# Prompt attention: scaled probabilities turned, values loaded for two heads and both groups, branches summed in PSUM, keys in four pieces

## The chip, the cores and the metric

One Trainium2 chip, one core. The metric is the device time of one execution in microseconds (us), as a median over runs; lower is better.

## The reference, cut to what matters

One inference step of a decoder layer on 1024 prompt tokens and 64 sample tokens. The part that changes is the sparse attention of the prompt: 8 query heads of width 64 in two groups of four, each group with its own keys and values, and three branches whose outputs are mixed with gates. With the top 16 of 16 blocks chosen, the selected branch of the prompt sees all earlier keys.

```python
def nsa_core(q, q_pos, kc, vc, ks_blk, vs_blk, kw, vw, kw_pos, gates, rel_bias):
    logit_c = einsum('bqgrd,bkgd->bgrqk', q, kc) * scale + bias      # 63 compressed keys
    p_c = masked_softmax(logit_c, dist_c >= 0)
    o_cmp = einsum('bgrqk,bkgd->bqgrd', p_c, vc)
    ...
    p_s = masked_softmax(logit_s, dist_s >= 0)                       # selected: all earlier keys
    o_slc = einsum('bgqnr,bgqnd->bqgrd', p_s, v_sel)
    ...
    p_w = masked_softmax(logit_w, mask_w)                            # window: the last 512 keys
    o_win = einsum('bgrqk,bkgd->bqgrd', p_w, vw)
    return gates[..., 0:1] * o_cmp + gates[..., 1:2] * o_slc + gates[..., 2:3] * o_win
```

The sum of the three is normalised and goes through an output projection that is added to x. Feed-forward layers, a state-space branch, a memory attention and the same attention for the sample tokens stand around it.

## The kernel before

The kernel is a row of stages, each a block of its own in which the five engines run side by side and at whose end they meet. `prompt_nsa_stage` stands between `scan_and_compress_stage` and `sample_nsa_stage`; after them comes `gemm_stage` "wout", the output projection that adds to x (`add_to=x`).

**Units.** The stage works in 8 tiles i of 128 queries. A unit u is one tile, one head (group g, head r of the group) and one branch b: b=0 is the selected branch over key tiles 0..i, b=1 the window branch over at most the last 5 key tiles, with the 63 compressed keys beside it. That makes 16 units a tile and 128 in all. Within a tile the order is head r, then group g, then branch b.

**A unit's path.** `scores(u)` on TensorE multiplies the packed queries by the keys split in a high and a low part (L2204, L2205) and adds biases with identity matmuls (L2211 near table, L2214 window mask, L2218 to L2222 compressed keys and their bias), into one of two halves of `s_ps`. VectorE takes the maximum (L2356, L2358). ScalarE takes the exponential with its sum (L2310, L2313) into `prob`, of which there are two. `turn(u)` transposes it by 128x128 pieces (L2233, L2236) into `t_ps`, of which there is one. ScalarE and VectorE copy it to `prob_t` (L2324 to L2329, L2369, L2371). `values(u)` multiplies: the turned probabilities are the loaded operand (128 columns), the values of one group move (64 columns), once for each key tile (L2251) and once for the compressed keys (L2255). The three branches of a head land side by side in `o_ps`. VectorE's `weights` forms gate/sum for the three, and `combine` scales and adds them into `o` (L2402, L2406). Once a tile, `turn_output` transposes `o` (L2264) and ScalarE copies it to `o_t` (L2334).

**Orders.** TensorE goes turn(u), scores(u+2), values(u-1); ScalarE exp(u+1), copy(u); VectorE maxima(u+1), copy(u), and after each b=1 unit weights and combine. Ahead of the first scores all tables and all keys are split (`to_split`, L2296 on ScalarE, L2420 on VectorE), and TensorE waits for the last of them. SyncE issues the loads: keys of the selected branch, near table, queries of tile 0, compressed bias, keys of the window branch, compressed keys, mask, queries of tile 1, then x itself (`x_back`: x had been put aside in DRAM, since its tile serves the scan stage), then further queries.

**The matmuls of `values`** are in plain fp32, and each of them stands in the trace as two records (a weight load and a matmul for each half of the operand). Those of `scores` are in the rounded fp32 type and stand as one.

## Time and profile before

| what | us |
|---|---|
| median of 3 runs (range) | 3262.19 (3257.46 to 3265.14) |
| the profiled execution, span from first to last instruction | 3261.7 |
| prompt attention, first scores to last output copy | 1542.9 to 1964.2 |
| TensorE busy in the whole span | 2881.9 (88%) |
| VectorE, ScalarE busy in the whole span | 1604.9 (49%), 983.2 (30%) |

The only time that the trace states for the profiled execution is its span, so the span stands for it. PE is TensorE's matmuls, PEld its weight loads, DVE VectorE, ACT ScalarE, SP SyncE. A busy PE is not a PE at its peak: matmuls overlap, so the distance between starts is read, not the duration of one. PEclk is the clock that was granted, 1.00 for 2.4 GHz and 0.50 for 1.2 GHz.

### The profile page before, as it was taken

The page shows a single profiled execution, that of the slowest core. Times are in us where ns is not written, and L with a number is a line of the kernel's source. Part 1 is how long each engine was busy: PE and PEld are TensorE (multiplying, and loading weights), DVE is VectorE, ACT ScalarE, POOL GpSimd, SP SyncE. Part 2 cuts the span into 40 slices and gives each one's busy share as a digit, 9 for nine tenths or more (in the row PEclk, how much of TensorE's full clock was granted, in tenths as well). Part 3 has the DMA queues.
Part 4 walks back from the last instruction along what each step waited for, and adds up shares of the span by engine and source line. Part 5 has one row for each costly group of instructions (what it writes and reads, how often), then busy time and mean ns, then how long its engine had stood idle before and what let it go on. Part 6 is the DMA issues. An engine that isn't in the chain of part 4 may idle for free. (4 is left out here: it accounts for less than half of the span.)

```text
span 3261.7 us, 49905 instructions
## 1 busy us (share of the span) xinstructions
PE 2881.9 (88%) x20104; PEld 2749.7 (84%) x20104; DVE 1604.9 (49%) x2976; ACT 983.2 (30%) x2029; POOL 117.4 (4%) x118
## 2 busy tenths in 40 slices
PE   5999999999799849994999995697475999999998
PEld 5999999999799849984999993496365999999997
DVE  6766766441631132433445552524337766666433
ACT  4333333211431221212344441412333333334111
POOL 5000000000000000000000000000005000000000
PEclk9999999999899966987579997798687999999999
DMA  2222224210342430204000005100201222224111
GB/s 85 80 80 78 73 77 148 106 67 1 111 54 58 151 112 12 72 27 147 20 14 8 1 1 147 40 27 27 88 19 39 75 77 74 77 80 174 67 67 56
DMA packets 121208, 221.37 MB, mean 68 GB/s; under 512 B 14388, under 2 KB 75860, under 8 KB 119508
## 3 DMA queue, kind: packets, MB, share of 16 engines
q1 hardware_dynamic: 116004, 207.88, 20.6%
q10 hardware_dynamic: 4976, 10.31, 0.8%
q8 instruction: 161, 2.64, 0.3%
q14 instruction: 67, 0.55, 0.1%
HBM read 172.85 MB, written 49.36 MB: 68 GB/s over the span
## 5 line engine op out<-in xcount | busy, mean ns | idle before, releaser
L740 PE MATMUL ffn_gate_up<-ffn_h_hi,ffn_w 128*128 128x272 f32 x1912 | 560.6, 293 | 60.4 <-DVE ffn_h_lo L881 42.0
L741 PE MATMUL ffn_gate_up<-ffn_h_lo,ffn_w 128*128 128x272 f32 x1912 | 558.0, 292 | 0.0
L742 PE MATMUL ffn_gate_up<-ffn_h_hi,ffn_w 128*128 128x272 f32 x1912 | 557.4, 292 | 0.0
L740 PEld LDWEIGHTS ffn_gate_up<-ffn_h_hi,ffn_w 128*128 128x128 f32 x1912 | 365.3, 191 | 65.8 <-DVE ffn_h_lo L881 32.0
L742 PEld LDWEIGHTS ffn_gate_up<-ffn_h_hi,ffn_w 128*128 128x128 f32 x1912 | 365.2, 191 | 0.0
L741 PEld LDWEIGHTS ffn_gate_up<-ffn_h_lo,ffn_w 128*128 128x128 f32 x1912 | 365.2, 191 | 0.0
L1073 DVE SCALAR_TENSOR_TENSOR x<-ffn_down,x 128x364 f32<-128x364 f32 (+1 forms) x240 | 126.1, 533 | 329.1 <-PE ffn_down L309 329.1
L886 DVE TENSOR_TENSOR ffn_w<-ffn_w_raw,ffn_w 128x512 fp32r<-128x512 f32 x264 | 186.6, 709 | 104.4 <-ACT ffn_w L621 104.4
L621 ACT ACTIVATE ffn_w<-ffn_w_raw 128x512 fp32r<-128x512 f32 x264 | 160.1, 625 | 99.3 <-PE ffn_down L742 79.2
L740 PE MATMUL ffn_down<-ffn_h_hi,ffn_w 128*128 128x272 f32 x552 | 163.7, 297 | 13.4 <-DVE ffn_w L886 7.9
L1479 PE MATMUL ssd_hid_ps<-ssd_pages,ssd_cmp_w 128*128 128x128 f32 (+1 forms) x1280 | 171.2, 298 | 0.0
L307 PE MATMUL mix_ps<-h_mix_hi,mix_w_hi 128*128 128x364 f32 x480 | 161.4, 336 | 9.4 <-issue 6.0
L1479 PEld LDWEIGHTS ssd_hid_ps<-ssd_pages,ssd_cmp_w 128*128 128x128 f32 x1280 | 163.8, 211 | 2.6
L741 PE MATMUL ffn_down<-ffn_h_lo,ffn_w 128*128 128x272 f32 x552 | 162.1, 294 | 0.0
L742 PE MATMUL ffn_down<-ffn_h_hi,ffn_w 128*128 128x272 f32 x552 | 161.9, 293 | 0.0
L309 PE MATMUL mix_ps<-h_mix_hi,mix_w_lo 128*128 128x364 f32 x480 | 160.0, 333 | 0.0
L308 PE MATMUL mix_ps<-h_mix_lo,mix_w_hi 128*128 128x364 f32 x480 | 160.0, 333 | 0.0
L2251 PE MATMUL pn_o_ps<-nat,pn_prob_t 128*128 128x64 f32 x1056 | 154.3, 294 | 0.0
L2251 PEld LDWEIGHTS pn_o_ps<-nat,pn_prob_t 128*128 128x128 f32 x1056 | 145.5, 212 | 0.0
L2310 ACT ACTIVATE pn_prob<-pn_s_ps,pn_neg_max 128x640 f32<-128x640 f32 (+7 forms) x128 | 89.9, 702 | 182.4 <-DVE pn_neg_max L2358 125.0
L307 PE MATMUL ffn_down<-ffn_h_hi 128*128 128x364 f32 (+1 forms) x384 | 126.2, 329 | 0.0
L309 PE MATMUL ffn_down<-ffn_h_hi,ffn_h_lo 128*128 128x364 f32 (+1 forms) x384 | 126.1, 328 | 0.0
(492 smaller groups left out, 6564.6 us busy)
## 6 DMA issues: line engine op xcount, KB each, us to landing
ffn_w_raw<-in_w_ffn_in SPq DMA_DIRECT2D x88, 512.0 KB, 4.1
scratch_ffn_act<-ffn_prod SPq DMA_DIRECT2D x88, 272.0 KB, 2.6
ffn_h_raw<-scratch_ffn_act SPq DMA_DIRECT2D x44, 544.0 KB, 7.2
mix_w_raw<-in_w_mix SPq DMA_DIRECT2D x20, 512.0 KB, 3.6
ffn_h_raw<-in_w_ffn_out SPq DMA_DIRECT2D x16, 512.0 KB, 9.1
ssd_pages<-in_cmp_pages SPq DMA_DIRECT2D x64, 128.0 KB, 2.2
sn_slc_pages<-in_slc_pages SPq DMA_DIRECT2D x64, 128.0 KB, 2.2
ffn_w_sum<-in_w_ffn_out SPq DMA_DIRECT2D x14, 512.0 KB, 11.1
```

What stands on the lines that cost most here:

```text
L307: pe.matmul(out, w_hi, x_hi, start=start, stop=False)
L308: pe.matmul(out, w_hi, x_lo, start=False, stop=False)
L309: return pe.matmul(out, w_lo, x_hi, start=False, stop=stop)
L621: act.activation(w[:, a, 0, :], fresh(a), ACT.Copy).then_inc(w_hi_ready, 1)
L740: pe.matmul(out, hi, x_hi, start=start, stop=False, skip_group_check=chained)
L741: pe.matmul(out, hi, x_lo, start=False, stop=False, skip_group_check=chained)
L742: mm = pe.matmul(out, lo, x_hi, start=False, stop=stop, skip_group_check=chained)
L886: dve.tensor_tensor(w[:, a, 1, :], fresh(a), w[:, a, 0, :].bitcast(F32), ALU.subtract).then_inc(w_ready, 1)
L1073: dve.scalar_tensor_tensor(xT[:, t, cols], dn_bank(d), 0.5, xT[:, t, cols], ALU.mult, ALU.add).then_inc(dn_added, 1)
L1479: mm = pe.matmul(hp[j % 2][:, 1 - later:1 - later + w].rearrange("p (b n) -> p b n", n=PAGES), w1s[:, kv, k, hh * P:(hh + 1) * P], pages[: ...
L2251: mm = pe.matmul(at, probt[:, u % 2, m * P:(m + 1) * P], nat[:, j, vcol:vcol + HEAD_DIM], start=m == 0, stop=m == len(kt) - 1)
L2310: e = act.activation(prob[:, u % 2, 0:w], s[:, 0:w], ACT.Exp, bias=neg_max[:, u % 2, 0:1], accum_out=sums[:, n % 2, 1 + b:2 + b])
```

## The change

It touches the prompt attention alone, and where x is loaded again.

- The probabilities of a unit are scaled by gate/sum on VectorE (`scale`: a reciprocal and a tensor_scalar with two per-row factors, for b=1 two of them) before they are turned. `weights`, `combine`, `o` and `turn_output` go.
- Eight units make a set: one tile, two heads r of each group, both groups, both branches. Turned probabilities of a set are kept in 14 slots (8 selected key tiles, 5 window key tiles, 1 compressed), in one of two buffers, the second of which is the tile of x.
- `values` loads the 64 columns of values of one group and moves 256 columns (two heads), for group 0 into PSUM partitions 0 to 63 and for group 1 into 64 to 127; all slots of a set add up in one PSUM tile. The matmuls of a set are issued in up to 7 portions behind the turns of the next set's units. ScalarE copies the finished set from `o_ps` into `o_t`.
- TensorE's order is scores(u+2), turn(u), portion; turn is cut in two with a signal each; VectorE takes maxima two units ahead. `prob` has three buffers. First copies of the turned pieces go to VectorE for b=0 units of group 0 and to ScalarE for the others, further pieces to ScalarE.
- Keys come and are split in four pieces of 256 tokens, the near table in two halves. The first scores wait for the first pieces alone, the second unit for the compressed tables, the second set for the second half of the near table. Queries are loaded into one buffer.
- `x_back` moves from the prompt stage's SyncE queue to the end of the sample stage's.

```diff
@@ prompt_nsa_stage: tiles @@
-        prob = sb("prob", [P, 2, 1024])
-        probt = sb("prob_t", [P, 2, 1024])
+        prob = sb("prob", [P, NB, 1024])
         neg_max = sb("neg_max", [P, 2, 2])
-        sums, rec, mix = sb("sums", [P, 2, 3]), sb("rec", [P, 2, 3]), sb("mix", [P, 2, 3])
-        o = sb("o", [P, 2, INNER])
-
+        sums, rec = sb("sums", [P, NB, 2]), sb("rec", [P, NB, 2])
...
+        half = SLOTS * 4 * P
+        own_probt = sb("prob_t", [P, half])
+        probt = [a.rearrange("p (n g r t) -> p n g r t", n=SLOTS, g=KV_GROUPS, r=2)
+                 for a in (own_probt[:], spare[:, 0:half])]
...
+        near_raw = spare[:, 0:H * 2 * P].rearrange("p (g v r c) -> p g v r c", g=KV_GROUPS, v=2, r=2)
...
+        def piece_at(u):
+            i, j = divmod(u, per_tile)
+            return (j // 8, (i + 1) // 2) if i % 2 and j % 8 == 2 and (i + 1) // 2 < PIECES else None
+        def key_piece(a, n, p):
+            return a[:, n, :].rearrange("p (g t) -> p g t", g=KV_GROUPS)[:, :, p * PIECE:(p + 1) * PIECE]
+        near_pair = lambda v: (near_raw[:, :, v], by_pairs(near_hi)[:, :, v], by_pairs(near_lo)[:, :, v])
+        NEAR0, EYE, CMPB, KC, WIN, NEAR1 = range(6)
+        tables = [(*near_pair(0), near_landed[0], 32), (core.ident, eye[:], None, None, 0),
+                  (cmpb, cmpb_hi[:], cmpb_lo[:], filled, 5), (kc_raw, kc_hi[:], kc_lo[:], kc_landed, 64),
+                  (win_raw, win[:], None, win_landed, 16), (*near_pair(1), near_landed[1], 32)]
+        split_count = {NEAR0: 1, CMPB: 2, KC: 3, NEAR1: 4}
...
+        has_rest = [len(key_tiles(u)) > 4 or units[u][3] == 1 for u in range(U)]
+        rests_before = [sum(has_rest[:u]) for u in range(U + 1)]
+        first_on_dve = [units[u][3] == 0 and units[u][1] == 0 for u in range(U)]
@@ sync @@
+                load_keys(0, 0)
+                load_q(0)
+                load_near(0)
+                load_keys(1, 0)
...
-                x_back(sp)
-                for i in range(2, tiles):
-                    load_q(sp, i)
+                load_near(1)
+                for i in range(1, tiles):
+                    load_q(i)
+                    if i % 2 and (i + 1) // 2 < PIECES:
+                        for n in range(2):
+                            load_keys(n, (i + 1) // 2)
@@ tensor @@
+                    if u % per_tile < 2 and i % 2 == 0:
+                        pe.wait_ge(k_ready[b], i // 2 + 1)
+                    if u == 0:
+                        pe.wait_ge(split_done, split_count[NEAR0])
+                        pe.wait_ge(hi_done, EYE + 1)
+                    if u == 1:
+                        pe.wait_ge(split_done, split_count[KC])
+                    if u == SET:
+                        pe.wait_ge(split_done, split_count[NEAR1])
+                        pe.wait_ge(hi_done, len(tables))
...
+                    pe.wait_ge(scaled, u + 1)
+                    if u:
+                        wait_first_copy(pe, u - 1)
...
-                    kt = key_tiles(u)
-                    at = o_ps[:, n % 2, (1 + b) * HEAD_DIM:(2 + b) * HEAD_DIM]
-                    vcol = b * P + g * HEAD_DIM
-                    for m, j in enumerate(kt):
-                        mm = pe.matmul(at, probt[:, u % 2, m * P:(m + 1) * P], nat[:, j, vcol:vcol + HEAD_DIM],
-                                       start=m == 0, stop=m == len(kt) - 1)
...
+                def values(s, steps, last):
+                    for n, (slot, b, j) in steps:
+                        for g in range(KV_GROUPS):
+                            gs = slice(g * HEAD_DIM, (g + 1) * HEAD_DIM)
+                            if b is None:
+                                vg = (DEC_BATCH * 2 + g) * HEAD_DIM
+                                v, keys = vc[:N_CMP, vg:vg + HEAD_DIM], N_CMP
+                            else:
+                                vg = b * P + g * HEAD_DIM
+                                v, keys = nat[:, j, vg:vg + HEAD_DIM], P
+                            mm = pe.matmul(o_ps[gs, s % 2, 0:2 * P], v,
+                                           probt[s % 2][:keys, slot, g].rearrange("p r t -> p (r t)"),
+                                           start=n == 0, stop=n == last)
+                    return mm
+                def some_values(s, k):
+                    slots = slots_of(s)
+                    steps = list(enumerate(slots))[len(slots) * (k - 1) // (SET - 1):len(slots) * k // (SET - 1)]
+                    if k == 1:
+                        pe.wait_ge(pt_act, act_copies[(s + 1) * SET])
+                        pe.wait_ge(pt_dve, dve_copies[(s + 1) * SET])
+                        if s >= 2:
+                            pe.wait_ge(o_done, s - 1)
+                    if steps:
+                        mm = values(s, steps, len(slots) - 1)
+                        if k == SET - 1:
+                            mm.then_inc(pv_ready, 1)
...
+                    turn(u)
+                    s, k = divmod(u, SET)
+                    if s and k:
+                        some_values(s - 1, k)
+                for k in range(1, SET):
+                    some_values(sets - 1, k)
@@ scalar @@
+                def take_output(s):
+                    i, v = divmod(s, 2)
+                    act.wait_ge(pv_ready, s + 1)
+                    act.activation(o_t[:, 2 * v:2 * v + 2, i * P:(i + 1) * P],
+                                   o_ps[:, s % 2, 0:2 * P].rearrange("p (r t) -> p r t", t=P), ACT.Copy
+                                   ).then_inc(o_done, 1)
...
+                    if u == 0:
+                        round_table(WIN)
+                        round_table(NEAR1)
+                    if u % SET == 0 and u >= 2 * SET:
+                        take_output(u // SET - 2)
@@ vector @@
+                def scale(u):
+                    i, g, r, b = units[u]
+                    h, w = g * GROUP_HEADS + r, len(key_tiles(u)) * P
+                    mine = prob[:, u % NB]
+                    dve.wait_ge(p_ready, u + 1)
+                    dve.reciprocal(rec[:, u % NB, 0:1 + b], sums[:, u % NB, 0:1 + b]).then_inc(rec_ready, 1)
+                    dve.wait_ge(rec_ready, u + 1)
+                    m = dve.tensor_scalar(mine[:, 0:w], mine[:, 0:w], rec[:, u % NB, 0:1], gates[:, i, h, 1 + b:2 + b],
+                                          ALU.mult, ALU.mult)
                     if b:
-                        w = min(n, 4) * P
-                        dve.tensor_copy(probt[:, u % 2, 0:w], t_ps[:, 0, 0:w]).then_inc(pt_dve, 1)
-                    elif n > 4:
-                        dve.tensor_copy(probt[:, u % 2, 4 * P:n * P], t_ps[:, 1, 0:(n - 4) * P]
-                                        ).then_inc(pt_dve, 1)
-                def weights(n):
-                    i, g, r, _ = units[2 * n]
-                    h = g * GROUP_HEADS + r
-                    dve.wait_ge(p_ready, 2 * n + 2)
-                    dve.reciprocal(rec[:, n % 2, :], sums[:, n % 2, :]).then_inc(rec_ready, 1)
-                    dve.wait_ge(rec_ready, n + 1)
-                    mixed = dve.tensor_tensor(mix[:, n % 2, :], rec[:, n % 2, :], gates[:, i, h, :], ALU.mult)
-                    if i == 0:
-                        mixed.then_inc(mix_ready, 1)
-                        dve.wait_ge(mix_ready, 2 * n + 1)
-                        mixed = dve.tensor_tensor(mix[:, n % 2, 0:1], mix[:, n % 2, 0:1], core.sees_cmp[:],
-                                                  ALU.mult)
-                    mixed.then_inc(mix_ready, 1)
...
-                def combine(n):
-                    i, g, r, _ = units[2 * n]
-                    at = o[:, i % 2, (2 * r + g) * HEAD_DIM:(2 * r + g + 1) * HEAD_DIM]
-                    dve.wait_ge(mix_ready, mix_count(n))
-                    dve.wait_ge(pv_ready, 2 * n + 2)
-                    if i >= 2:
-                        dve.wait_ge(ot_ps, i - 1)
-                    for k in range(3):
-                        part = o_ps[:, n % 2, k * HEAD_DIM:(k + 1) * HEAD_DIM]
-                        if k == 0:
-                            dve.tensor_scalar(at, part, mix[:, n % 2, 0:1], None, ALU.mult
-                                              ).then_inc(part_ready, 1)
-                        else:
-                            dve.wait_ge(part_ready, 2 * n + k)
-                            dve.scalar_tensor_tensor(at, part, mix[:, n % 2, k:k + 1], at, ALU.mult, ALU.add
-                                                     ).then_inc(part_ready if k == 1 else o_ready, 1)
+                        own = mine[:, 5 * P:5 * P + N_CMP]
+                        m = dve.tensor_scalar(own, own, rec[:, u % NB, 1:2], gates[:, i, h, 0:1], ALU.mult, ALU.mult)
+                    m.then_inc(scaled, 1)
...
+                maxima(1)
+                scale(0)
                 for u in range(U):
                     if u % per_tile == pack_at and u + per_tile < U:
                         pack(units[u][0] + 1)
+                    if piece_at(u):
+                        rest_keys(*piece_at(u))
+                    if u + 2 < U:
+                        maxima(u + 2)
+                    copy(u)
+                    if u == 0:
+                        rest_table(NEAR1)
                     if u + 1 < U:
-                        maxima(u + 1)
-                    copy(u)
-                    if units[u][3]:
-                        weights(u // 2)
-                        if u > 1:
-                            combine(u // 2 - 1)
-                combine(U // 2 - 1)
+                        scale(u + 1)
@@ sample_nsa_stage, sync, and trunk @@
                for bt in range(PAIRS):
                    load(bt)
+                x_back(sp)
...
+            prompt_nsa_stage(core, nat, kc, vc, o["proj"], rows, o_t, x[:].rearrange("p k t -> p (k t)"))
+            sample_nsa_stage(core, nat, kc, vc, o["proj"], rows, i["rules"], i["page_table"],
+                             i["slc_pages"], i["win_kv"], gates_dram, o_t, n_pool,
```

## Rows read from the trace of the kernel before

**Rows 1.** The page: the granted clock in 40 slices of 81.5 us, in tenths:

```profile
PEclk9999999999899966987579997798687999999999
```

**Rows 2.** Windows of the prompt attention: length, busy (records), PEclk, DMA share, GB/s; sum of ten:

```profile
1578.00:1626.00 48.00, 47.22 (x216) 44.97 (x216) 20.68 (x76) 17.55 (x69) 0.00 (x0) 0.50 0.05 12
...
1674.00:1724.00 50.00, 47.04 (x364) 43.84 (x364) 30.64 (x89) 24.48 (x77) 0.00 (x0) 1.00 0.05 12
...
sum 454.00, PE 412.27 PEld 391.25 DVE 234.91 ACT 190.51 POOL 1.48; mean PE 41.23 PEld 39.12 DVE 23.49 ACT 19.05 POOL 0.15
```

**Rows 3.** Groups in the stretch 1480 to 2060: busy us, mean ns, idle before:

```profile
L2251 PE MATMUL pn_o_ps<-nat,pn_prob_t 128*128 128x64 f32 x1056 | 154.3, 294 | 0.0
...
L2233 PE MATMUL pn_t_ps<-const_all,pn_prob 128*128 128x128 f32 x528 | 92.6, 302 | 8.6 <-ACT mixed L2334 5.5 <-ACT pn_prob L2313 2.2 <-issue 0.7
L2356 DVE TENSOR_REDUCE pn_neg_max<-pn_s_ps 128x1 f32<-128x640 f32 (+7 forms) x128 | 90.1, 704 | 64.3 <-PE pn_s_ps L2211 61.5 <-PE pn_s_ps L2222 2.3
...
L2369 DVE COPY pn_prob_t<-pn_t_ps 128x512 f32<-128x512 f32 (+3 forms) x64 | 37.8, 591 | 85.1 <-PE pn_t_ps L2236 85.1
L2406 DVE SCALAR_TENSOR_TENSOR pn_o<-pn_o_ps,pn_mix,pn_o 128x64 f32<-128x64 f32 x128 | 36.3, 284 | 4.6
L2324 ACT ACTIVATE pn_prob_t<-pn_t_ps 128x512 f32<-128x512 f32 (+3 forms) x64 | 33.1, 517 | 4.1 <-PE pn_t_ps L2233 3.7
L2255 PE MATMUL pn_o_ps<-vc,pn_prob_t 63*128 63x64 f32 x128 | 32.7, 343 | 0.0
...
L2402 DVE TENSOR_SCALAR pn_o<-pn_o_ps,pn_mix 128x64 f32<-128x64 f32 x64 | 18.1, 284 | 1.7 <-PE pn_o_ps L2255 1.4 <-DVE pn_mix L2381 0.3
...
L2264 PE MATMUL pn_t_ps<-const_all,pn_o 128*128 128x128 f32 x32 | 5.8, 312 | 1.1 <-DVE pn_o L2406 1.1
```

**Rows 4.** The values in the slow stretch, by line:

```profile
1542.00:1674.00 132.00, 40.40 (x155) 37.86 (x156) 0.50 0.13 39
```

**Rows 5.** Timeline of TensorE in tile 7, clock 1.00: start, length, records:

```profile
1949.67 1.22 PE L2251 MATMUL pn_o_ps<-nat,pn_prob_t 128*128 128x64 f32 x10
1950.82 0.43 PE L2255 MATMUL pn_o_ps<-vc,pn_prob_t 63*128 63x64 f32 x2
1951.18 0.77 PE L2233 MATMUL pn_t_ps<-const_all,pn_prob 128*128 128x128 f32 x5
```

**Rows 6.** Timeline of TensorE in the memory attention, clock 0.50:

```profile
2340.38 0.41 PE L3027 MATMUL ma_s_ps<-ma_k_lo,ma_q_prompt 128*128 128x256 f32 x1
2340.73 1.98 PE L3047 MATMUL ma_o_ps<-ma_prob_t,ma_v 128*64 128x128 f32 x16
```

**Rows 7.** Windows around 512-column matmuls in the sample attention:

```profile
2008.00:2010.00 2.00, 1.96 (x12) 0.58 (x16) 0.00 (x0) 0.00 (x0) 0.00 (x0) 0.50 0.52 147
2012.00:2014.00 2.00, 2.00 (x23) 0.93 (x21) 0.00 (x0) 0.00 (x0) 0.00 (x0) 1.00 0.42 134
```

**Rows 8.** Timeline of the start of the prompt attention:

```profile
1515.27 2.47 SPq L2151 DMA_DIRECT2D pn_raw<-out_proj  x4
...
1522.68 1.91 ACT L2296 ACTIVATE pn_k_hi<-pn_raw 128x2048 fp32r<-128x2048 f32 x1 [17.66 <-DMA pn_raw<-out_proj]
...
1542.92 0.44 PE L2204 MATMUL pn_s_ps<-pn_k_hi,pn_q 128*128 128x128 f32 x1 [31.63 <-DVE pn_cmp_bias_lo L2420]
```

**Rows 9.** VectorE groups by shape, whole span:

```profile
L234 DVE SCALAR_TENSOR_TENSOR wout_norm_normed<-mixed,inner_gains,wout_norm_inv_rms 128x364 f32<-128x364 f32 x24 | 13.8, 595 | 0.6
...
L2784 DVE TENSOR_SCALAR sn_prob<-sn_prob,sn_mix 128x1088 f32<-128x1088 f32 x4 | 3.1, 786 | 0.1
...
L2785 DVE TENSOR_SCALAR sn_prob<-sn_prob,sn_mix 128x576 f32<-128x576 f32 x4 | 2.1, 513 | 0.0
```

**Rows 10.** DMA issues: count, KB each, us to landing:

```profile
x<-scratch_x SPq DMA_DIRECT2D x1, 4368.0 KB, 17.3
```

**Rows 11.** Timeline of SyncE, the last load of the sample attention:

```profile
2042.06 0.43 SPq L2532 DMA_DIRECT2D sn_win_kv<-in_win_kv  x1
```

**Rows 12.** Timeline of VectorE, the first use of x:

```profile
2125.62 0.98 DVE L1198 TENSOR_TENSOR x<-wout_ps,x 128x364 f32<-128x364 f32 x2
```

More of the change, by code:

```diff
@@ L2105, in prompt_nsa_stage @@
         U = len(units)
+        SET = 2 * KV_GROUPS * 2
+        sets = U // SET
+        per_tile = 2 * H
+        pack_at = 6
         def key_tiles(u):
@@ new lines, in prompt_nsa_stage, with rest_copies @@
+        has_rest = [len(key_tiles(u)) > 4 or units[u][3] == 1 for u in range(U)]
+        rests_before = [sum(has_rest[:u]) for u in range(U + 1)]
+        first_on_dve = [units[u][3] == 0 and units[u][1] == 0 for u in range(U)]
+        dve_copies = [sum(first_on_dve[:u]) for u in range(U + 1)]
+        def rest_copies(u):
+            n, b = len(key_tiles(u)), units[u][3]
+            return (n > 4) + b
+        act_copies = [0]
+        for u in range(U):
+            act_copies.append(act_copies[-1] + (not first_on_dve[u]) + rest_copies(u))
@@ new lines, in wait_first_copy, with slots_of, turned @@
+        def wait_first_copy(pe, u):
+            if first_on_dve[u]:
+                pe.wait_ge(pt_dve, dve_copies[u + 1])
+            else:
+                pe.wait_ge(pt_act, act_copies[u] + 1)
+        def slots_of(s):
+            slc, own = key_tiles(s * SET), key_tiles(s * SET + 1)
+            return [(m, 0, j) for m, j in enumerate(slc)] + [(WIN0 + m, 1, j) for m, j in enumerate(own)] + \
+                [(CMP_SLOT, None, None)]
+        def turned(u, first, count, keys=P):
+            i, g, r, b = units[u]
+            base = (WIN0 if b else 0) + first
+            return probt[u // SET % 2][:keys, base:base + count, g, r % 2, :]
@@ L2225, in turn @@
                 def turn(u):
-                    pe.wait_ge(p_ready, u + 1)
-                    pe.wait_ge(pt_act, act_copies[u])
-                    pe.wait_ge(pt_dve, dve_copies[u])
-                    if u % per_tile == turn_at + 1 and units[u][0]:
-                        pe.wait_ge(ot_ready, units[u][0])
-                    for n in range(len(key_tiles(u))):
-                        mm = pe.transpose(t_ps[:, n // 4, (n % 4) * P:(n % 4 + 1) * P],
-                                          prob[:, u % 2, n * P:(n + 1) * P], core.ident[:])
@@ L2269, in _ @@
-                pe.wait_ge(split_done, splits)
+                    b, n = units[u][3], len(key_tiles(u))
+                    pe.wait_ge(scaled, u + 1)
+                    if u:
+                        wait_first_copy(pe, u - 1)
+                    for m in range(min(n, 4)):
+                        mm = pe.transpose(t_ps[:, 0, m * P:(m + 1) * P], prob[:, u % NB, m * P:(m + 1) * P],
+                                          core.ident[:])
+                    mm.then_inc(t_first, 1)
+                    if not has_rest[u]:
+                        return
@@ L2272, in _ @@
                 for u in range(U):
-                    turn(u)
                     if u + 2 < U:
                         scores(u + 2)
-                    if u:
-                        values(u - 1)
-                    if u % per_tile == turn_at and units[u][0]:
-                        turn_output(units[u][0] - 1, u)
-                values(U - 1)
-                turn_output(tiles - 1, U - 1)
+                    turn(u)
[4 more added lines that the diff above has]
+                    some_values(sets - 1, k)
             @block.scalar
@@ L2298, in _ @@
                                ).then_inc(gates_ready, 1)
+                round_keys(0, 0)
+                pack(0)
+                round_table(NEAR0)
+                round_table(EYE)
+                round_keys(1, 0)
                 def exp(u):
-                    i, g, r, b = units[u]
-                    n = u // 2
+                    b = units[u][3]
                     w = len(key_tiles(u)) * P
@@ L2344, in _ @@
                     copy(u)
-                    if u % per_tile == turn_at and units[u][0]:
-                        take_output(units[u][0] - 1)
-                take_output(tiles - 1)
+                    if u == 0:
[3 more added lines that the diff above has]
+                        take_output(u // SET - 2)
+                take_output(sets - 2)
+                take_output(sets - 1)
             @block.vector
```

243 lines of the change are left out of this document (116 added, 127 removed).

## Prediction

> **What bounds the kernel now.** I read the granted clock of the page first [rows 1]. The prompt attention (1543 to 1964) fills the 20th to the 24th of the 40 digits: 5, 7, 9, 9, 9. The stage began at the low clock and kept it for a third of its length (until 1674, near the end of tile 2). The windows say what TensorE did then [rows 2]: in 1578 to 1626 it was busy for 47.2 of 48 us, with 216 matmul records at 0.50; in 1674 to 1724 it was busy for 47.0 of 50 us with 364 at 1.00. So TensorE is never short of work, at either clock, and its own instructions set the stage's length. The other engines are well below: in the ten windows the sums are 412 us for PE, 235 for DVE, 191 for ACT [rows 2]. The groups say what PE does [rows 3]: the values are the largest, 1056 records (L2251) and 128 for the compressed keys (L2255), ahead of 528 transposes. The timelines give the distances that the sum needs: at 1.00 ten values records and the step to the next take 1.15 us, so 0.112 us each [rows 5], though only 64 columns move, with a load of 128 columns before each. Two kinds of waste stand there, a weight load as dear as the matmul, and a low clock.
>
> **Values.** Before: of 1056 records 155 run at 0.50 [rows 4]. The distance there I take as 0.213 us, twice 0.107: the window at 0.50 has 216 records of all kinds in 48 us, 0.22 each [rows 2]. 155 x 0.213 + 901 x 0.112 = 134 us. The compressed keys are another tile shape (63 rows); their groups' busy time, 32.7 us [rows 3], is near what they occupy, since a pair in tile 7 takes 0.36 us (1950.82 to 1951.18) [rows 5] and one at the low clock about twice that. Together 167 us.
>
> After: 3 + 5 + 7 + 9 + 11 + 12 + 13 + 14 = 74 slots a set pair, 148 in all, each with two matmuls (one a group) of 256 columns, four records. What does such a record cost? The trace has the very shape, also with neighbours in different halves of the array's columns: the memory attention's 16 records of 128*64 with 128 columns take 1.98 us at 0.50 [rows 6]. Less a last record's 0.42 that is (1.98 - 0.42) / 7 = 0.22 us for two of them. Twice the columns at twice the clock cost the same, so 0.22 us (I take 0.218) for a pair at 1.00 and 0.43 at 0.50, if the halves work side by side at 256 columns as they do there. Six slots of tile 0 run at 0.50 (12 pairs x 0.43 = 5 us), 142 at 1.00 (284 x 0.218 = 62 us): 67 us.
>
> The change adds a price: each portion of values changes the array's shape from 128*128 to 128*64 and back. Going from 128*128 scores to 128*64 values took 0.35 us from start to start (2340.38 to 2340.73), 0.13 more than a plain step, at 0.50 [rows 6]; a 63-row pair at 1.00 costs 0.36 instead of 0.22, 0.14 for going in and out less what overlaps [rows 5]. There are 3 + 5 + 6 x 7 = 50 portions for each of two sets, 100, so 200 changes; at 0.1 us (bounds 0 and 0.13) 20 us, and 2 for the compressed slot. The Trainium skill has a rule against this change: by TensorEngine Tiling (Array Packing), Key Properties, changing the tiling mode, not merely the tile, drains the engine. It gives no figure, so by the rule alone the term is a loss of unknown size; the 0.13 us of the row agrees.
>
> Values after: 67 + 22 = 89. **Gain 167 - 89 = 78 us.**
>
> **Output turns.** `turn_output` goes: 5.8 us busy and 5.5 us in which transposes waited for the ACT copy [rows 3]. **Gain 10 us** (bounds 6 and 11).
>
> **Clock.** 131 us ran at 0.50 (1543 to 1674), 33 of them values, 14 compressed values (20 pairs at 0.7), 3 output turns; about 81 are scores and transposes. Tile 0 of these is 15 records a unit pair x 8 pairs x 0.213 = 26 us. What did the engine do before its clock rose? Elsewhere it rose within 4 us of full-length 512-column matmuls in quarter tiles (0.50 at 2008, 1.00 at 2012) [rows 7]; in this stage it stayed low through nearly all of tiles 0 to 2, where most matmuls have 64 to 256 columns and each waits for its weight load. Afterwards the values have 256 columns in two halves at once, and they begin with unit 9, in tile 0. I take it that the clock rises some 8 us into tile 1. Then (81 - 26 - 7) / 2 = 24 us are saved. **Gain 24 us**; bounds 0 (rises as late as now) and 40 (rises in tile 0).
>
> **Start.** TensorE's first scores began at 1542.92, 31.6 us after its last work, released by the last table split; the first key load was issued at 1515.27 and its 1 MB landed at 1522.7 [rows 8]. Now the first scores need a quarter of the keys, the queries and half the near table: four instead of nine loads' worth of bytes, about 1527. But unit 1 waits for the compressed bias tables, which still come behind these (about 1531), and at u = 0 ACT and DVE have the second half of the near table in their queues, whose load is issued last, near 1530, and lands some 8 us later as such loads do. Behind it stand exp(2) and scale(1), so turn(1) stalls until about 1539 with only about 5 us of work done ahead. The stage is then 9 us ahead of before. **Gain 9 us** (bounds 4 and 13). The later key pieces (ACT and DVE, two of each every second tile) are the same columns as before, now under TensorE.
>
> **VectorE and ScalarE.** `scale`: 786 ns for 1088 columns, 513 for 576 [rows 9], so 0.206 + 0.533 ns a column. The units have 8 x 128 x (36 + 30) = 67,584 columns in all: 128 x 0.206 + 36 = 62 us, 64 short ones at 0.25 = 16, 128 reciprocals at 0.17 = 21: 99 us. Removed: 36.3 + 18.1 [rows 3] and some 22 of reciprocals and mixes. Copies fall from 37.8 [rows 3] and 16 of a smaller group to 19 us, since only 32 units' first copies (mean 0.59) stay. Net about -11, so 224 us. ACT gets 32 more first copies (0.517 each [rows 3]), 32 further ones and 16 outputs (some 0.4 each) for 8 outputs now, about +32: 223 us. Both have to fit in some 310 us of TensorE. They fit, but no longer loosely, and they are chained: `t_ps` and the two halves of `s_ps` are single per role. In a light tile (tile 1 at 1.00) a pair of units takes PE 2.8 us and DVE about 2.6. I add **10 us of stalls** (bounds 0 and 35, the latter if scaling with two per-row factors goes one column a ns, as a two-input operation does: 364 columns in 595 ns [rows 9], which makes DVE 36 us longer).
>
> **x.** `x_back` took 17.3 us to land [rows 10], issued behind the last sample load (2042.06 [rows 11]); it lands about 2060, the first use is at 2125.6 [rows 12]. 65 us of slack: cost 0. Without that slack it would be 17.
>
> **Sum.** 78 + 24 + 10 + 9 - 10 = 111 us from a span of 3261.7, which is 0.5 below the median of 3262.2. **Forecast 3151.**
>
> **Rivals.**
> 1. The clock rises as late as now, near the end of tile 2. For it: transposes and bias matmuls of at most 256 columns are untouched and make up most of the records. Price: the 24 us, and the 24 slots of tiles 1 and 2 at twice 0.44, 10 more: 3185. 17%.
> 2. VectorE becomes the pace-setter in the light tiles by the slow scaling. Price 15 to 25: 3171. 12%.
> 3. The halves don't overlap at 256 columns. Against it: the 128x64 rows [rows 6]. Price 284 x 0.218 = 62 and 5: 3218. 5%.
> 4. Slower: the clock never rises in the stage. Stalls, shape changes and small matmuls keep it at 0.50 to the end. The stage after is 421 - 111 + 9 = 319 us, of which some 270 at 1.00; at 0.50 they take up to 270 more, less 35 of stalls that vanish and shape changes that don't double: about 3385. It decides once 220 us of work at 1.00 turn slow. Against it: today's stage, with nothing wider in its first tiles, does rise. 5%.
>
> **How the numbers follow.** Forecast 59% (3125 to 3175), rivals 17, 12, 5, 5, something that leaves the time about as it is 2. The range of 8 in 10 reaches down to an early rise and no cost of shape changes (16 and 20 us, 3115) and up over rivals 1 and 2 together (3205). Faster by over 0.2% 0.93, within 0.2% (6.5 us, about what three such runs can tell from no change) 0.02, slower 0.05.
>
> **What would show it.** Values records fall to 592, in pairs started together, 0.22 us apart at 1.00. PEclk reads 0.50 in tile 0 and 1.00 from about 1590. DVE and ACT each about 225 us in the stage. The stage ends near 1853 instead of 1964. Gap to the first scores about 15 us, with a second gap until about 1539. L1198 waits for PE, not for x. Wrong if: PEclk stays at 0.50 past tile 1, pairs stand 0.43 apart at 1.00, TensorE waits for `scale` more than 10 us in all, or wout waits for the x load.

## The result, and the profile after

| | us |
|---|---|
| after, median of 4 runs (range) | 3167.47 (3163.2 to 3173.43) |
| before, median of 4 runs (range) | 3261.59 (3257.46 to 3265.14) |
| after / before | 0.9711, 95% interval 0.9698 to 0.9725 |

The kernel is 94 us faster; the forecast was 111, in its range. The profiled execution of after has a span of 3171.7, the longest of its four, 90.0 below that of before.

The page: totals, and the granted clock in 40 slices of 79.3 us, beside [rows 1]:

```profile
PE 2803.2 (88%) x19480; PEld 2611.3 (82%) x19480; DVE 1598.8 (50%) x2912; ACT 1000.2 (32%) x2108; POOL 117.4 (4%) x118
...
PEclk9999999999899976898699987896678999999999
```

Groups of the stage (1520 to 1868), beside [rows 3]: busy us, mean ns, idle before and its releasers.

```profile
L2284 PE MATMUL pn_t_ps<-const_all,pn_prob 128*128 128x128 f32 x416 | 72.5, 287 | 11.6 <-DVE pn_prob L2463 11.2 <-DVE pn_prob L2459 0.2
L2459 DVE TENSOR_SCALAR pn_prob<-pn_prob,pn_rec,pn_gates 128x640 f32<-128x640 f32 (+7 forms) x128 | 71.0, 555 | 4.7
...
L2309 PE MATMUL pn_o_ps<-pn_prob_t,nat 128*64 128x256 f32 x264 | 39.8, 405 | 0.0
...
L2309 PE MATMUL pn_o_ps<-x,nat 128*64 128x256 f32 x264 | 37.5, 395 | 0.0
...
L2457 DVE RECIPROCAL pn_rec<-pn_sums 128x1 f32<-128x1 f32 (+1 forms) x128 | 19.8, 155 | 1.1 <-ACT pn_prob L2378 0.9
L2463 DVE TENSOR_SCALAR pn_prob<-pn_prob,pn_rec,pn_gates 128x63 f32<-128x63 f32 x64 | 19.7, 308 | 0.0
```

The values, 187 us of busy records before [rows 3], are 264 + 264 records here and 64 more for the compressed keys. In exchange the transposes wait for `scale` (L2459, L2463), 11.4 us in all.

Windows tile by tile, from one tile's first exponential to the next: length, busy (records) of PE, PEld, DVE, ACT and POOL, PEclk, DMA share, GB/s. Tiles 1 and 2 of before, then tiles 0 to 2 and the sum of all eight of after:

```profile
1579.80:1628.00 48.20, 47.42 (x216) 45.17 (x215) 20.67 (x74) 17.26 (x67) 0.00 (x0) 0.50 0.05 12
1628.00:1683.30 55.30, 54.24 (x265) 52.06 (x265) 23.78 (x73) 19.91 (x66) 0.00 (x0) 0.58 0.05 10
```

```profile
1528.50:1563.60 35.10, 29.86 (x129) 25.78 (x130) 18.52 (x70) 16.21 (x72) 0.41 (x2) 0.50 0.24 54
1563.60:1591.70 28.10, 23.47 (x166) 17.43 (x165) 20.78 (x71) 18.43 (x74) 0.00 (x0) 0.99 0.16 39
1591.70:1623.70 32.00, 29.34 (x201) 21.85 (x199) 23.52 (x70) 20.16 (x72) 0.00 (x0) 1.00 0.07 17
...
sum 337.40, PE 319.11 PEld 241.98 DVE 222.75 ACT 201.63 POOL 0.41; mean PE 39.89 PEld 30.25 DVE 27.84 ACT 25.20 POOL 0.05
```

Nearly half of the gain, 43.4 us, comes from tiles 1 and 2 (103.5 to 60.1): they were at the low clock, tile 2 until near its end [rows 2], now they are not. There TensorE now idles, 4.6 and 2.7 us of them, where it was idle for 0.8 and 1.1. The tiles of all kernels (tile 7 up to the end of the last values, in the kernels with the old order up to the last output turn behind them; names as in the experiments below):

```
us of tile            0     1     2     3     4     5     6     7   PEclk, tile 1
before              35.4  48.1  55.4  43.4  54.0  55.9  59.5  67.4   0.50
after               35.1  28.1  32.0  37.2  46.1  47.5  50.3  60.7   0.99
3 portions          35.3  31.1  32.8  40.4  45.0  47.8  48.7  59.5   0.87
1 portion           35.7  31.7  33.5  39.8  45.9  50.3  49.7  58.1   0.79
same half           35.4  30.2  36.2  42.6  53.9  57.3  61.0  79.6   1.00
no scale            35.6  24.8  29.1  34.6  45.0  46.5  49.2  59.2   0.99
fill after          35.0  28.2  32.0  37.2  46.1  47.5  50.2  60.6   0.99
fill before         33.7  41.5  58.7  43.4  54.0  55.9  59.5  67.4   0.66
wait all            30.1  32.5  32.0  37.2  46.1  47.5  50.2  60.6   0.71
one slot            33.0  30.4  32.8  37.2  46.1  47.5  50.2  60.6   0.78
portion first       35.8  31.0  31.6  37.2  45.7  46.8  48.7  58.1   0.89
before, few values  35.4  37.2  37.4  44.8  54.0  55.9  59.5  67.4   0.70
first from tile 4   35.3  28.1  32.0  37.2  46.2  46.8  48.7  58.1   1.00
the same, 4 portions 35.3 32.5  32.0  37.2  46.1  49.8  49.2  58.5   0.76
```

The timeline of TensorE in tile 7 of after, around one portion (start, length, records), beside [rows 5]:

```profile
1819.98 0.27 PE L2292 MATMUL pn_t_ps<-const_all,pn_prob 128*128 128x128 f32 x1
1820.09 0.27 PE L2295 MATMUL pn_t_ps<-const_all,pn_prob 128*63 128x128 f32 x1
1820.29 1.08 PE L2309 MATMUL pn_o_ps<-x,nat 128*64 128x256 f32 x8
1821.31 0.50 PE L2256 MATMUL pn_s_ps<-pn_k_hi,pn_q 128*128 128x512 f32 x1
1821.64 0.39 PE L2257 MATMUL pn_s_ps<-pn_k_lo,pn_q 128*128 128x512 f32 x1
1821.87 0.40 PE L2256 MATMUL pn_s_ps<-pn_k_hi,pn_q 128*128 128x512 f32 x1
1822.11 0.39 PE L2257 MATMUL pn_s_ps<-pn_k_lo,pn_q 128*128 128x512 f32 x1
```

Two transposes stand 0.11 apart, the last one and the first values 0.20: 0.09 for going in. The last portions of the stage stand together, with nothing between them, and show the pair's own price:

```profile
1859.29 5.57 PE L2309 MATMUL pn_o_ps<-x,nat 128*64 128x256 f32 x50
```

(5.57 - 0.38) / 24 = 0.216 us a pair, as forecast. Four such pairs are 0.86; in the portion they take 1.02 (1820.29 to 1821.31), 0.16 more. What the way out costs shows only beside a turn that has no portion behind it, the first of a set:

```profile
1810.53 0.60 PE L2292 MATMUL pn_t_ps<-const_all,pn_prob 128*128 128x128 f32 x4
1810.89 0.48 PE L2256 MATMUL pn_s_ps<-pn_k_hi,pn_q 128*128 128x512 f32 x1
1811.20 0.40 PE L2257 MATMUL pn_s_ps<-pn_k_lo,pn_q 128*128 128x512 f32 x1
```

The four transposes start 0.11 apart, so the last of them at 1810.86 and the first scores only 0.03 behind it. From the last transpose to the second scores matmul it is 0.34 us here, and 1.55 with a portion of four pairs between them (1820.09 to 1821.64). Less 0.86 for the pairs, a portion so costs 0.35 us beside its pairs: 0.09 going in, 0.16 within, 0.10 going out. The forecast had 0.20.

The start and x, from the timeline of after, beside [rows 8, 11, 12]:

```profile
1527.05 0.45 PE L2256 MATMUL pn_s_ps<-pn_k_hi,pn_q 128*128 128x128 f32 x1 [14.96 <-DVE pn_near_bias_lo L2480]
...
1531.48 0.45 PE L2256 MATMUL pn_s_ps<-pn_k_hi,pn_q 128*128 128x128 f32 x1 [3.34 <-DVE pn_kc_lo L2480]
...
1537.75 0.48 PE L2284 MATMUL pn_t_ps<-const_all,pn_prob 128*128 128x128 f32 x1 [1.17 <-DVE pn_prob L2463]
...
1943.82 0.43 SPq L3251 DMA_DIRECT2D x<-scratch_x  x1
...
2030.47 0.54 DVE L1198 TENSOR_TENSOR x<-wout_ps,x 128x364 f32<-128x364 f32 x1
```

x is issued at 1943.8 and lands 14.3 us later, 72 us before its first use; nothing waits for it. The stage's last output copy ends at 1865.9 instead of 1964.2, 98 us earlier. The other 8 us are given back in later stages that the change does not touch: the sample attention (from here to its last combine) takes 111.9 us instead of 107.9, with TensorE's mean clock at 0.69 instead of 0.73, the output projection 0.8 and what follows up to the feed-forward layer 2.7 us more. In eight of the ten other kernels that load x at the new place the sample attention takes 107.3 to 109.3, so its 4.0 us belong to this execution, not to x.

### The profile page after: what moved, and what is told of

The parts are those of the page before. It is cut to its first block and busy times, and to the rows that moved or that the text cites. A ratio compares the mean times of both kernels' runs of the same rounds, so it can differ in the third digit from the quotient of the medians.

```text
span 3171.7 us, 48273 instructions
## 1 busy us (share of the span) xinstructions
PE 2803.2 (88%) x19480; PEld 2611.3 (82%) x19480; DVE 1598.8 (50%) x2912; ACT 1000.2 (32%) x2108; POOL 117.4 (4%) x118
## 5 line engine op out<-in xcount | busy, mean ns | idle before, releaser
L2435 DVE TENSOR_REDUCE pn_neg_max<-pn_s_ps 128x1 f32<-128x640 f32 (+7 forms) x128 | 90.4, 706 | 88.1 <-PE pn_s_ps L2263 49.0
L308 PE MATMUL ffn_down<-ffn_h_lo,ffn_h_hi 128*128 128x364 f32 (+1 forms) x384 | 126.1, 328 | 0.0
L2024 DVE TENSOR_TENSOR mix_w_lo<-mix_w_raw,mix_w_hi 128x1024 fp32r<-128x1024 f32 (+1 forms) x22 | 27.2, 1234 | 190.0 <-ACT mix_w_hi L1958 190.0
```

What stands on the lines that cost most here:

```text
L308: pe.matmul(out, w_hi, x_lo, start=False, stop=False)
L2024: dve.tensor_tensor(w_lo[:, n % 2, 0:w], raw[:, n % 2, 0:w], w_hi[:, n % 2, 0:w].bitcast(F32), ALU.subtract).then_inc(lo_ready, 1)
L2435: m = dve.tensor_reduce(neg_max[:, u % 2, 0:1], s[:, 0:w], AX_X, ALU.max, negate=True)
```

## Experiments

Each ratio is to the kernel before on the same chip; 0.9711 is the changed kernel's own. 0.001 is 3.3 us.

**3 portions a set** (48 instead of 100) and **1 portion a set** (16):

```diff
-  steps = ...[len(slots) * (k - 1) // (SET - 1):len(slots) * k // (SET - 1)]
+  if k not in PORTIONS: return              # (3, 5, 7), or (4,)
+  at, count = PORTIONS.index(k), len(PORTIONS)
+  steps = ...[len(slots) * at // count:len(slots) * (at + 1) // count]
```

> The changed kernel with the values of each set issued in 3 portions (behind the 4th, 6th and 8th unit of the next set) instead of up to 7: 48 portions instead of 100. Theory A, the shape changes are what the forecast undersized: in the profile of the changed kernel the step from a transpose to a values matmul and back costs some 0.09 us each way and the scores matmul behind it another 0.1, so 0.29 us a portion instead of the 0.20 of the forecast; 52 portions fewer give 15 us, so about 3152 us. Theory B, the missing time is stalls in the chain of maxima, exponential, scale and turn: larger portions change nothing there, or lengthen it, so 3160 to 3175 us. Were a shape change free, the same 3167.

> The changed kernel with all values of a set in one portion, behind the 5th unit of the next set: 16 portions instead of 100. Theory A: 84 portions fewer at 0.29 us give 24 us, so about 3143 us, if VectorE and ScalarE keep enough work ahead while TensorE is in a portion of 3 to 6 us. Theory B: the portion leaves both without work, then TensorE waits for them in turn; 1 to 2 us for each of 16 portions are lost again and the time is 3155 to 3170 us.

Measured 3171.39 us, 0.9734 (0.9715 to 0.9752), and 3176.64 us, 0.9750 (0.9734 to 0.9766): one portion is slower than the changed kernel, three portions are at best as fast (the intervals overlap; in its profile the stage, counted from its first scores, is 3.7 us longer). Both gains that theory A gave are missing. Yet the price is there. The last two tiles with 3 portions (windows, to be laid beside 50.3 and 49.59, 61.1 and 59.64 of after):

```profile
1759.00:1807.70 48.70, 47.27 (x355) 38.42 (x354) 33.61 (x69) 30.81 (x89) 0.00 (x0) 1.00 0.00 1
1807.70:1867.50 59.80, 57.61 (x445) 44.21 (x444) 33.46 (x69) 33.28 (x92) 0.00 (x0) 1.00 0.00 1
```

TensorE is busy 2.3 and 2.0 us less for 8 portions fewer in each, 0.25 to 0.29 us apiece. It is given back as waiting: TensorE waits for `scale` 16.0 us instead of 11.4 and for the exponential 8.5 instead of 2.9; tiles 4 to 7 are 3.6 us shorter, but tile 3 is 3.2 us longer; and tile 1, where the clock fell again (PEclk 0.87, and 0.79 with 1 portion), 3.0. A small portion costs a change of shape and gives TensorE work while VectorE scales; fewer portions save the one and lose the other.

**Both groups in the same half.**

```diff
-  mm = pe.matmul(o_ps[gs, s % 2, 0:2 * P], v, ..., start=n == 0, stop=n == last)
+  mm = pe.matmul(o_ps[0:HEAD_DIM, s % 2, g * 2 * P:(g + 1) * 2 * P], v, ...,
+                 start=n == 0 and g == 0, stop=n == last and g == 1)
```

ScalarE then takes a set out in two copies instead of one.

> The changed kernel with the values matmuls of both groups in the same half of the columns (both accumulate in partitions 0 to 63 of one PSUM bank, side by side), and two ScalarE copies a set instead of one. Same numbers of instructions and columns on TensorE. Theory (the forecast's): the two halves work side by side, and this takes it away: each pair takes 0.43 us instead of 0.22 at the full clock, 284 pairs and 12 at the low clock give 62 + 5 = 67 us more, about 3232 us; less (some 50 us more) where TensorE waited in the light tiles anyway. Rival (the matmuls overlap by their loads, wherever they write): no change, 3167.

Measured 3227.26 us, 0.9903 (0.9888 to 0.9919): by the ratios 63 us more than the changed kernel, by the medians 60. The timeline of its last portion:

```profile
1921.73 5.99 PE L2309 MATMUL pn_o_ps<-x,nat 128*64 128x256 f32 x27
```

27 records in 5.99 us, so (5.99 - 0.38) / 13 = 0.43 a pair against 0.216. The halves work side by side, and about two thirds of the whole gain hang on where the second group writes.

**No scale.**

```diff
 def scale(u):
     dve.wait_ge(p_ready, u + 1)
-    ...                                       # reciprocal, one or two tensor_scalar
 def turn(u):
-    pe.wait_ge(scaled, u + 1)
+    pe.wait_ge(p_ready, u + 1)
```

> The changed kernel without scaling: the probabilities are turned as the exponential left them, not divided by their sum and not weighted by the gates; the turn waits for the exponential alone. That takes some 100 us of VectorE work and one link out of the chain. Theory A (stalls on scale are a real part of the miss): the 14 us in which TensorE waited for scale go, and the time falls by 10 to 15 us, to 3152 to 3157. Theory B (the waits only move to the next link: exponential, copy): it falls by less than 5 us. In tiles 5 to 8, where TensorE has no gaps, nothing may change.

Measured 3159.08 us, 0.9694 (0.9673 to 0.9714), 5.5 us below the changed kernel with intervals that touch; in its profile the stage ends 12.6 us earlier, after a start 0.2 later. All waits for `scale` are gone, those for the exponential stay at 3 us:

```profile
1564.30:1589.10 24.80, 22.81 (x166) 17.28 (x165) 11.72 (x31) 18.41 (x73) 0.00 (x0) 0.99 0.18 43
1589.10:1618.20 29.10, 28.97 (x202) 21.84 (x200) 13.17 (x29) 20.26 (x72) 0.00 (x0) 1.00 0.08 19
```

Tiles 1 to 3 are 3.3, 2.9 and 2.6 us shorter, tiles 4 to 7 by 1.0 to 1.5 each. TensorE is then busy for 28.97 of 29.10 us in tile 2: the chain through VectorE costs the stage 13 us, as theory A has it, though only the profile resolves it.

**Fillers in the changed kernel** and **in the kernel before**: matmuls of 512 columns into a free bank while TensorE waits for the tables.

```diff
+  fill(20); scores(0); fill(5); scores(1)      # changed kernel
+  fill(50)                                     # kernel before, ahead of its first wait
```

> The changed kernel with filler matmuls (512 columns each, of data that is there, into a PSUM bank not yet in use) on TensorE ahead of the first scores (20) and between the first and the second unit's scores (5), in which time TensorE has nothing else to do for 12 and 3.5 us. Theory A: the low clock of the stage's first 37 us (until 1564) comes from TensorE's idle time and its short matmuls; fillers bring the clock up, and tile 0 (35 us long, TensorE busy for 30 of them) gets 5 to 12 us shorter, until VectorE and ScalarE (21 us each) and the chain set the pace, so 3155 to 3162 us. Theory B: the short matmuls of tile 0 bring the clock down again within it: under 5 us gained, or none, 3163 to 3169.

> The kernel before with 50 such filler matmuls in the 31 us that TensorE waits ahead of the first scores; nothing else changed. If the fillers bring the clock up and it stays up, the 131 us at the low clock become some 70 and the time falls by 40 to 60 us, to about 3205: then a good part of the change's gain was to be had from the clock alone. If the clock falls again in tile 0 or 1, as its rows until 1674 suggest (TensorE busy 47.2 of 48 us at the low clock and no rise), the time falls by 0 to 10 us. I hold the second for likelier.

Measured 3172.79 us, 0.9737 (0.9716 to 0.9757), and 3277.21 us, 1.0057 (1.0037 to 1.0078). A filler took 0.9 us, where I had planned for 0.6, so the first exponential came 6.6 and 14.9 us late. The clock did come up: in the changed kernel (windows)

```profile
1519.60:1535.10 15.50, 15.50 (x41) 7.13 (x40) 4.27 (x6) 4.23 (x6) 0.51 (x2) 1.00 0.95 244
1535.10:1543.40 8.30, 6.67 (x31) 4.07 (x29) 3.78 (x9) 3.79 (x12) 0.00 (x0) 0.99 0.02 5
1543.60:1570.10 26.50, 24.79 (x108) 21.15 (x109) 14.44 (x61) 12.33 (x60) 0.00 (x0) 0.50 0.09 21
```

it stayed for 8 us of tile 0 and fell again for the rest; tile 0 took its 35.0 us all the same. In the kernel before it fell at 1562, 3 us into tile 0, and tiles 1 and 2 ran at 0.66 and 0.54; of the late start 5 us were won back. So theory B of both: the low clock in these tiles goes with the work in them; taking away the pause ahead did not keep it up.

**Before, with few values.** `kt = key_tiles(u)[:1]` in `values` for tiles 0 to 2.

> The kernel before with only the first key tile of each unit's values in tiles 0 to 2 (the rest of these tiles' values is left out, so their output is not the attention's): 48 matmuls fewer, 96 records, 20 us of them at the low clock's 0.213 us. Theory A: it is these matmuls of 64 moving columns behind loads of 128 that hold the clock at 0.50 until 1674; with most of them gone it rises in tile 1, and the time falls by the 20 us and 25 to 40 more, to 3200 to 3215 us. Theory B: the clock stays low through tiles 1 and 2 all the same (the transposes and short bias matmuls hold it): only the 20 us go, 3240 us.

Measured 3239.02 us, 0.9934 (0.9911 to 0.9957), 21.5 us less. Theory A was right on the clock and theory B on the time (windows of tiles 1 and 2):

```profile
1581.40:1618.70 37.30, 33.45 (x189) 31.62 (x188) 20.38 (x75) 16.66 (x67) 0.00 (x0) 0.70 0.07 15
1618.70:1656.10 37.40, 28.46 (x203) 26.79 (x203) 23.11 (x73) 18.98 (x68) 0.00 (x0) 0.95 0.07 15
```

With these matmuls left out, PEclk is 0.70 and 0.95 instead of 0.50 and 0.58. But in tile 2 TensorE then idles for 9 of 37.4 us, most of it for the exponential:

```profile
PE pn_t_ps L2233 <- ACT pn_prob L2313: 7.9, 6, 2.5
```

VectorE is busy for 23.1 us there and ScalarE for 19.0, so neither is full: it is the chain of maximum, exponential and turn that TensorE meets. A higher clock is worth only as much as this chain leaves.

**One slot of values in tiles 0 and 1 of the changed kernel.** `slots_of(s)[:1 if s < 4 else SLOTS]`.

> The changed kernel with only the first slot of the values of the first four sets (tiles 0 and 1), the other 12 slots left out, so that the output of these two tiles is not the attention's. Everything else on TensorE stays. Theory A: it is the values with 256 moving columns in two halves that bring the clock up at 1564, 110 us earlier than before. Without them it stays at 0.50 through tile 1 (28 us long at 1.00, some 42 at 0.50) and into tile 2, and the stage ends 10 to 25 us later although work is left out: 3175 to 3190 us. Theory B: the clock rises at about 1564 whatever the values do (by the earlier start, the other order of work, or by itself); then only the left out pairs are missing, 24 x 0.22 to 0.43 = 5 to 8 us, 3160 us.

Measured 3166.98 us, 0.9712 (0.9694 to 0.9731). Theory B for the most part: the clock rises in tile 1 with most of the wide values left out, but some 8 us later (0.50 in 1562.6 to 1572.2, 1.00 from there to 1585.9) and not firmly (PEclk 0.78 and 0.95 in tiles 1 and 2 instead of 0.99 and 1.00), and that eats the 5 to 8 us of the work left out. With the run before it this points to the old 64-column matmuls as what held the clock down, more than to the new ones as what brings it up; the order and the start differ too, so their share stays open.

**All tables ahead of the first scores.** The waits of `scores(0)`, `scores(1)` and `scores(SET)` all stand at u = 0; ScalarE and VectorE split every table first.

> The changed kernel, but the first scores wait for every table (all of them are split ahead of the first unit's exponential), as in the kernel before; keys still come in pieces. Theory A (the early start is worth what the profile shows, the first exponential at 1528.5 instead of 1544.4): the second half of the near table lands at 1534.5 and is split by 1537, so the first scores begin 10 us later, the stall of 1.2 us behind unit 1 goes, and the stage ends 7 to 9 us later: 3175 us. Theory B (the forecast's: most of the early start is given back by stalls before 1539): 1 to 4 us later.

Measured 3176.95 us, 0.9743 (0.9723 to 0.9762), 10 us above the changed kernel. First scores 10.6 us later (1537.6), tile 0 5.0 shorter (its stalls are gone), tile 1 4.4 longer with PEclk 0.71. So of the 10 us 5.6 are the start's own, and 4.4 depend on when the clock rises. That may be chance: the run with 4 portions below, with the changed kernel's own code in tile 1, takes the same 32.5 us there.

**Portion ahead of the turn**, everywhere, **from tile 4 on**, and there **with 4 portions**:

```diff
   scores(u + 2)
+  if s and k: some_values(s - 1, k)
   turn(u)
-  if s and k: some_values(s - 1, k)
```

> The changed kernel with a portion of values issued ahead of the turn of its unit instead of behind it (scores of unit u+2, portion, turn of unit u). Same instructions, same number of shape changes. Theory A (the turn waits for scale because scale has only the scores' time to run in): the portion covers it, the gap of 0.5 us a set in tiles 4 to 7 and most of 2.5 to 3.3 us in each of tiles 1 to 3 go, and the time falls by 6 to 12 us, near what leaving scale out gave (12.7 us of the stage in its profile). Theory B: VectorE and ScalarE then get the turned pieces later, so that copies and the next scores wait instead: within 4 us of the changed kernel, either side.

> The changed kernel with the portion of values ahead of the turn in tiles 4 to 7 only, and behind it, as in the changed kernel, in tiles 0 to 3. The run with the portion first everywhere had tiles 4 to 7 shorter by 0.4, 0.7, 1.6 and 2.6 us and tile 1 longer by 2.9 (6.7 us of it at the low clock). Theory: both are properties of the order in those tiles, so the stage is 5 us shorter than the changed kernel's and the time about 3162 us, 2 below the run with the portion first everywhere. Rival: tile 1's length is the chance of when the clock rises; then nothing is gained over that run and both are 3163 to 3167.

> The same with 4 portions a set instead of 7 in tiles 4 to 7 (behind no other change): 24 portions fewer. With the portion ahead of the turn a portion costs 0.24 us of shape changes in the profile: 6 us less. A turn without a portion ahead waits for scale about 0.5 us, as the first turn of each set does: 24 of them, 12 us more, less what a longer portion covers. Theory A (stalls win, as they did with 3 portions): 0 to 6 us slower than with seven, 3162 to 3168. Theory B (TensorE has the most work in these tiles, VectorE and ScalarE under 0.75 busy, so the stalls are hidden): 3 to 6 us faster, 3157 to 3160.

Measured 3163.79 us, 0.9702 (0.9683 to 0.9720); 3159.51, 0.9706 (0.9687 to 0.9725); 3168.13, 0.9724 (0.9707 to 0.9741). The waits of TensorE in the first of these runs (portion first everywhere):

```profile
PE pn_s_ps L2256 <- ACT pn_prob L2378: 10.0, 20, 1.3
...
PE pn_t_ps L2284 <- DVE pn_prob L2463: 1.2, 1, 1.2
```

and of the changed kernel:

```profile
PE pn_t_ps L2284 <- DVE pn_prob L2463: 11.2, 21, 1.2
...
PE pn_s_ps L2256 <- ACT pn_prob L2378: 2.9, 4, 1.0
```

The wait has moved from `scale` to the exponential, as theory B said. Tiles 4 to 7 are 0.4, 0.7, 1.6 and 2.6 us shorter all the same, and with the order changed there alone the second run repeats this in tiles 5 to 7, while tiles 0 to 3 are those of the changed kernel; its stage is 4.6 us shorter. Most of what the heavy tiles gain is a lower price of a portion. The timeline of the second run, first a turn without a portion ahead of it, then one with two pairs:

```profile
1806.29 0.28 PE L2263 MATMUL pn_s_ps<-pn_near_bias_lo,pn_eye 128*128 128x256 f32 x1
1806.41 0.60 PE L2284 MATMUL pn_t_ps<-const_all,pn_prob 128*128 128x128 f32 x4
1806.85 0.60 PE L2292 MATMUL pn_t_ps<-const_all,pn_prob 128*128 128x128 f32 x4
...
1808.86 0.28 PE L2274 MATMUL pn_s_ps<-pn_cmp_bias_lo,pn_eye 128*128 128x64 f32 x1
1809.07 0.65 PE L2309 MATMUL pn_o_ps<-x,nat 128*64 128x256 f32 x4
1809.65 0.66 PE L2284 MATMUL pn_t_ps<-const_all,pn_prob 128*128 128x128 f32 x4
1810.14 0.27 PE L2292 MATMUL pn_t_ps<-const_all,pn_prob 128*128 128x128 f32 x1
```

From the last scores to the fifth transpose it is 0.56 us without and 1.28 with the portion; less 0.43 for its two pairs a portion costs 0.29, against 0.35 behind the turn. For 56 portions in tiles 4 to 7 that is some 3 us, and TensorE's waits there fall from 2.9 to 1.9: together 4 of the 4.8 us that these tiles gain. By the ratios, 0.9702 and 0.9706 against 0.9711, neither run can be told from the changed kernel. Four portions were no gain: tile 5 is 3.0 us longer, and tile 1, whose code is the same as in the run beside it, took 32.5 instead of 28.1 us at PEclk 0.76. When the clock rises is thus not settled by the code of the stretch alone, and a scatter of 4.4 us can come from it; how much of the changed kernel's own does, its one profile does not show.

## Why the prediction was right or wrong

Of the 111 us forecast, the stage gave 98 and the span 90 (the medians 94).

- **Values.** 0.218 us a pair was forecast, 0.216 measured; the same-half run bears out the overlap and its 62 + 5 us (63 measured), so rival 3 is out. **The step that was off is "200 changes; at 0.1 us (bounds 0 and 0.13) 20 us".** Two changes cost 0.35. The last set's seven portions stand together, which leaves 94, so 33 us: 13 too little. The row behind 0.13 showed the way in; it did not show what the pairs of a portion lose (0.16 in all) and what the way out costs (0.10). The Trainium skill's rule, that a change of the tiling mode drains the engine (TensorEngine Tiling (Array Packing), Key Properties), had the right sign, with no figure; the runs agree with it, by 0.35 us for both ways.
- **Output turns.** Gone; nothing in the tiles speaks against 10, and no run tested it.
- **Clock.** The term had the rise 8 us into tile 1 (which the text puts at 1590; with tile 1 beginning at 1563.6 it would have been 1572). It rose with tile 1, at 1564. The term was 24 us; 8 us at the full instead of the half clock are 4 more. That it rose so early is luck in part, since with the same code in tile 1 another run had it 16 us into the tile. The reason given, that 256 columns in two halves bring it up, held in part at most: it rises with most of them left out too, 8 us later and less firmly, and leaving out the old 64-column values brings it up in the kernel before. Rival 1 did not come, but the wait-all and 4-portion runs show a piece of it, 4.4 us.
- **Start.** First scores at 1527.05 and unit 1 at 1531.48, as forecast; `turn(1)` stood still only until 1537.8, for 1.2 us. At the start of tile 1 the kernel is 16.2 us ahead; 9 for the start had been forecast, and by the forecast's prices some 8 for tile 0's values. Right within 1 in sum.
- **VectorE and ScalarE.** The forecast counted from 1510 to the end of the stage; there after has 227.8 and 208.0 us, against 224 and 223: VectorE 4 more, ScalarE 15 less. `scale` costs 110.5 instead of 99: 0.28 us and 0.52 ns a column fit its groups, so the base was too low (by the rows of 1088 and 576 columns, [rows 9]) and the slope right. The slow scaling of rival 2 did not come, but part of its effect did, the waits for `scale`.
- **Stalls.** 10 forecast; the waits for `scale` and the exponential are 14.3 us where before had 2.2 for the exponential, 12 net, and leaving scale out shortens the stage by 12.8. The waits for `scale` alone, 11.4, are over the 10 us that "wrong if" had named.
- **x.** Cost 0, right.

Together: 111, less 13 for the changes of shape, 2 for stalls and 1 for the start, plus 4 by the clock, is 99; the stage gave 98. The last 8 of the profile (some 4 of the median) are scatter of later stages. The time landed at 3167, nearer rival 2's 3171 than the forecast's 3151, but not by rival 2's mechanism: the largest part is a term that the forecast named and priced too low.

## What to carry to other kernels

Count excursions into another tile shape, and price each with both ways and the first matmul behind it; a row that shows one way gives less than half. Before spending that price away with fewer, larger portions, see what the small ones cover: here they hid VectorE, and merging them lost what it saved, or more. Try the other place in the order, too: the same portion cost 0.35 us behind the turn and 0.29 ahead of it. And hold the gain of a tile against what the chain through the other engines leaves in that same tile, not in the whole stage.

## What was not expected of the hardware

- One excursion from 128*128 to 128*64 and back cost 0.35 us at the full clock between transposes and scores, and 0.29 between scores and transposes.
- Wide filler matmuls brought the clock to 1.00, but it fell again 3 us (kernel before) and 8 us (changed kernel) after the first exponential, under the short matmuls of tile 0.
- With the same instructions in tiles 0 to 3, the clock rose at the start of tile 1 in one kernel's profile and half a tile later in another's.
